# Four modulation chunks on ScalarE's queue, constants in two transfers, and matmuls in TensorE's early waits

## The reference

```python
mod = silu_c @ w_ada[l] + b_ada[l]
mod_ctx = silu_cc @ w_ada[l] + b_ada[l]
sh1, sc1, g1, sh2, sc2, g2 = jnp.split(mod[:, None, :], N_ADA, axis=-1)
...
u_ctx = _modulate(_rms_norm(ctx, norm1_g[l]), sh1c, sc1c)
hc_f, hc_b = _bidir_rglru(u_ctx @ w_in[l][:, :D_LRU], *lru_p, h_zero, h_zero)
...
u = _modulate(_rms_norm(x, norm1_g[l]), sh1, sc1)
mix, _, _ = _mixer(u, rows, h0_f, h0_b, w_in[l], ...)
x = x + g1 * mix
x = x + g2 * _swiglu(_modulate(_rms_norm(x, norm2_g[l]), sh2, sc2), w_ffn_in[l], w_ffn_out[l])
return _rms_norm(x, norm_f_g)
```

## Time and profile before

| | us |
|---|---|
| median of three runs | 2579.61 |
| the profiled execution's own time | 2582.47 |
| its span, first to last instruction | 2580.7 |
| TensorE busy in the span | 2552.7 (99%) |
| VectorE busy | 1983.7 (77%) |
| ScalarE busy | 1220.8 (47%) |

### The profile page before, as it was taken

How to read it: one execution, slowest core, us unless ns; L and a number is a source line. 1 busy time by engine, 2 the same in 40 slices (tenths; PEclk the granted TensorE clock), 3 DMA queues, 4 the chain that set the end, 5 groups by cost and what they waited for, 6 DMA issues and landing times.

```text
span 2580.7 us, 39175 instructions
## 1 busy us (share of the span) xinstructions
PE 2552.7 (99%) x14527; PEld 2197.5 (85%) x14527; DVE 1983.7 (77%) x2223; ACT 1220.8 (47%) x1422; POOL 205.5 (8%) x277
## 2 busy tenths in 40 slices
PE   7999999999999999999999999999999999999998
PEld 6888888878888888888888888888888888888887
DVE  5567998778999999877967878777877767787443
ACT  4224887355555555422444444444444445455433
POOL 0010000000001111111000000000000000011000
PEclk8999999999999999999999999999999999999999
DMA  9985444755556666999668888888888864756644
GB/s 353 355 316 187 131 132 150 270 198 159 159 162 160 166 156 149 323 334 337 176 156 203 203 199 204 202 201 200 205 202 200 207 236 148 164 125 179 218 158 153
DMA packets 540412, 524.81 MB, mean 203 GB/s; under 512 B 16472, under 2 KB 491424, under 8 KB 535584
## 3 DMA queue, kind: packets, MB, share of 16 engines
q1 hardware_dynamic: 491296, 379.17, 47.8%
q0 software_dynamic: 44176, 126.90, 21.0%
q10 hardware_dynamic: 4848, 17.47, 1.7%
HBM read 427.00 MB, written 54.53 MB: 187 GB/s over the span
## 4 chain that ended last, share of the span: by engine, by line
PE 93%; DVE 3%; DMA 2%; ACT 1%; issue 1%; ACTq 0%; SPq 0%; DVEq 0%
PE main L1758 17%; PE aux L1758 17%; PE main L1765 9%; PE aux L1765 9%; PE main L1471 7%; PE main L1472 7%; PE main L1473 7%; PE aux L1999 3%; PE aux L1998 3%; PE aux L2000 3%; DMA ada_pa<-in_w_ada 1%; PE aux L1521 1%; PE main L1999 1%; PE main L2000 1%; PE main L1998 1%; PE aux L1471 1%
## 5 line engine op out<-in xcount | busy, mean ns | idle before, releaser
L2478 DVE TENSOR_TENSOR l_S<-f_S,h_S 128x1024 fp32r<-128x1024 f32 x288 | 344.9, 1219 | 15.3 <-ACT h_S L1056 15.3
L2478 DVE TENSOR_TENSOR l_A<-f_A,h_A 128x1024 fp32r<-128x1024 f32 x216 | 263.3, 1221 | 101.8 <-ACT h_A L1056 87.8
L1056 ACT ACTIVATE h_A<-f_A 128x1024 fp32r<-128x1024 f32 x216 | 226.6, 1051 | 221.2 <-PE aux L1765 111.6
L1056 ACT ACTIVATE h_S<-f_S 128x1024 fp32r<-128x1024 f32 x288 | 288.8, 1052 | 72.6 <-DVE f_S L2466 47.3
L1471 PE MATMUL main<-u_both,w_hi 128*128 128x512 f32 (+1 forms) x528 | 207.9, 394 | 0.3 <-DVE ctx_lo L2213 0.2
L1758 PE MATMUL main<-t_both,h_S 128*128 128x512 f32 x864 | 207.9, 389 | 0.2 <-DVE u_hi_spare L2531 0.2
L1758 PE MATMUL aux<-t_both,h_S 128*128 128x512 f32 x864 | 207.8, 389 | 0.0
L1472 PE MATMUL main<-u_both,w_hi 128*128 128x512 f32 (+1 forms) x528 | 203.7, 386 | 0.0
L1473 PE MATMUL main<-u_both,w_lo 128*128 128x512 f32 (+1 forms) x528 | 203.1, 385 | 0.0
L2126 DVE TENSOR_TENSOR w_lo<-w_raw,w_hi 128x1024 fp32r<-128x1024 f32 x120 | 146.0, 1221 | 64.7 <-ACT w_hi L826 64.5
L826 ACT ACTIVATE w_hi<-w_raw 128x1024 fp32r<-128x1024 f32 x120 | 125.8, 1053 | 147.6 <-DMA w_raw<-in_w_out 60.9
(11 more groups left out here) (363 smaller groups left out, 5637.1 us busy)
## 6 DMA issues: line engine op xcount, KB each, us to landing
f_A<-in_w_ffn_in SPq DMA_DIRECT2D x120, 512.0 KB, 5.3
f_S<-in_w_ffn_in SPq DMA_DIRECT2D x80, 512.0 KB, 5.7
f_S<-f_A POOLq DMA_DIRECT2D x80, 512.0 KB, 6.4
f_A<-in_w_in SPq DMA_DIRECT2D x72, 512.0 KB, 4.9
ada_pq<-in_w_ada SPq DMA_DIRECT2D x64, 512.0 KB, 8.5
ada_pw<-in_w_ada POOLq DMA_DIRECT2D x64, 512.0 KB, 6.2
bw_f<-in_w_ffn_out SPq DMA_DIRECT2D x56, 512.0 KB, 7.1
w_raw<-in_w_in SPq DMA_DIRECT2D x48, 512.0 KB, 4.7
```

The costliest lines, as they stand in the source:

```text
L1056: act.activation(wh[v][:, :, :], wf[b][v][:, :, :], ACT.Copy).then_inc(w_hi_done, 1)
L2478: dve.tensor_tensor(wl[b][v][:, :, :], wf[b][v][:, :, :], wh[v][:, :, :].bitcast(F32), ALU.subtract).then_inc(w_lo_done, 1)
```

## The change

**Chunks.** The first four chunks no longer come through GpSimd's queue into `ada2_pa`. ScalarE issues their transfers, before `hi` of unit 8, as soon as the last piece is used, into a new tile `ada2_pl` over the second half of the ring of pieces. GpSimd issues chunks 4 to 31, the first four of them without waiting for a free slot. VectorE takes chunks 0 to 3 from `ada2_pl`; the edges of `pad` rows 4 to 7 are cleared, and those rows written, only after chunk 3 is used.

**Constants.** The identity (64 KB) is loaded first; the other 256 KB are loaded by SP just ahead of the store of x. Their readers wait for the second transfer.

**Matmuls in the waits.** `keep_warm(n)` issues n float32 matmuls of 256 columns into a free accumulator; nobody reads what they write. Nine stand among pieces 3, 4 and 5.

```diff
--- before.py
+++ after.py
@@ -59,7 +59,7 @@
 EARLY_CHUNKS = {8: 5, 9: 5, 10: 5, 11: 5, 12: 4, 13: 4, 14: 4, 15: 0}
 N_EARLY = 32
 N_MID = N_EARLY + 16
-LANDED = (20 * 16, 20 * 16, 12 * 16, 12 * 16)
+LANDED = (19 * 16, 19 * 16, 11 * 16, 11 * 16)
 
 
 NPAIR = D_FF // P
@@ -249,6 +249,7 @@
         xcv_l = sb("xcv_l", "ada", [TCAT], F32R, 3 * kb)
         dft_t = sb("dft_t", "mix", [3, T], F32, 16 * kb)
         ada2_pa = sb("ada2_pa", "yx", [4, 1024])
+        ada2_pl = sb("ada2_pl", "lru", [4, 1024], F32, 16 * kb)
         ada2_pc = sb("ada2_pc", "pf", [2, 1024])
         ada2_pw = sb("ada2_pw", "u_hi", [4, 1024], F32, 16 * kb)
         ada2_acc = sb("ada2_acc", "ada", [1024], F32, 8 * kb)
@@ -437,7 +438,7 @@
                 unit(0, 8, 0, u, in_t[:, UC * q:UC * q + UC, j * UN:j * UN + UN])
 
 
-            sp.dma_start(const[:, :], consts).then_inc(const_landed, 16)
+            sp.dma_start(const[:, 0:P], consts[:, 0:P]).then_inc(const_landed, 16)
             for i in range(4):
                 sp.dma_start(x_tok[:, i, :], x[0, P * i:P * i + P, :]).then_inc(rows_landed[i], 16)
             for i in range(2):
@@ -447,6 +448,7 @@
                 for u in EARLY_UNITS.get(n, ()):
                     xa_unit(u)
             sp.wait_ge(raw_out, 16)
+            sp.dma_start(const[:, P:], consts[:, P:]).then_inc(const_landed, 16)
             sp.dma_start(x_fm, x_raw[:, :, :]).then_inc(x_stored, 16)
             for u in range(8, 16):
                 xa_unit(u)
@@ -756,8 +758,8 @@
 
             pool.wait_ge(x_stored, 16)
             pool.wait_ge(u_aff, 2 * KT)
-            for n in range(N_EARLY):
-                if n >= 4:
+            for n in range(4, N_EARLY):
+                if n >= 8:
                     pool.wait_ge(ada2_used, n - 3)
                 chunk(n, ada2_pa[:, n % 4, :])
             for n in range(N_EARLY, N_MID):
@@ -889,6 +891,9 @@
                 act.activation(pad[:, 4 * i + 2 * j:4 * i + 2 * j + 2, PADX:PADX + T], main[:, 2 * j:2 * j + 2, :],
                                ACT.Copy).then_inc(pair_free[j], 1)
 
+            act.wait_ge(ada_used, 32)
+            for n in range(4):
+                act.dma_start(ada2_pl[:, n, :], ada_t[:, n, 2 * D:2 * D + 1024]).then_inc(ada_landed[n], 16)
             hi(0, 8, 0, 8)
             hi(0, 8, 0, 9)
             xa_out(0, 0)
@@ -896,6 +901,7 @@
             for u in range(8, 16):
                 hi(0, 8, 0, u + 2)
                 if u % 4 == 3:
+                    act.wait_ge(ada2_used, 4)
                     xa_out(1, u // 4 - 2)
             sums_evac(2, 2, sums_row)
 
@@ -1590,10 +1596,22 @@
             ins.then_inc(rstd_spread, 1)
             pe.wait_ge(cvec_ready, 1)
 
-            for n in range(4):
+            pe.wait_ge(raw_out, 24)
+
+            def keep_warm(n):
+
+                for _ in range(n):
+                    pe.matmul(main[:, 3, 0:256], ones[:, :], x_raw[:, 0, 0:256], start=True, stop=True)
+
+            for n in range(3):
                 ada_piece(n)
+            keep_warm(3)
+            ada_piece(3)
+            keep_warm(1)
             turn_row(0)
+            keep_warm(2)
             ada_piece(4)
+            keep_warm(3)
             for n in range(5, 32):
                 ada_piece(n)
                 xa_half(n - 5, n // 4 if n % 4 == 3 else None)
@@ -1664,12 +1682,14 @@
             def middle_channels():
 
                 pe.wait_ge(branch_out, 4)
+                pe.wait_ge(const_landed, 32)
                 for g in range(4):
                     ins = pe.matmul(aux[0:1, 3, g * P:g * P + P], yx[:, 12 + g, TH:TH + 1], cs128[:, 0:P], start=True, stop=True)
                 ins.then_inc(chunk_ready, 1)
 
             def channels(t):
                 pe.wait_ge(side_rows_done, 5)
+                pe.wait_ge(const_landed, 32)
                 pe.wait_ge(branch_out, 7 + t)
                 for g in range(4):
                     for odd in range(2):
@@ -1680,7 +1700,7 @@
 
             def tokens(t):
                 if t == 0:
-                    pe.wait_ge(const_landed, 64)
+                    pe.wait_ge(const_landed, 80)
                     pe.wait_ge(row_out, len(RANGES) + 2)
                 pe.wait_ge(pair_free[t], Q_FOUR // 2 + 1)
                 for g in range(4):
@@ -2136,9 +2156,12 @@
                     ins = dve.scalar_tensor_tensor(acc[:, :], src, k, acc[:, :], ALU.mult, ALU.add)
                 ins.then_inc(ada2_used, 1)
 
-            def chunk_next(n, src, acc=None):
-                dve.wait_ge(ada2_landed[n % 4], 16 * (n // 4 + 1))
-                chunk(src, n, cvec[:, n % 16, 0:1], acc)
+            def chunk_next(n, acc=None):
+                if n < 4:
+                    dve.wait_ge(ada_landed[n], 32 * 8 + 16)
+                else:
+                    dve.wait_ge(ada2_landed[n % 4], 16 * (n // 4))
+                chunk(ada2_pl[:, n, :] if n < 4 else ada2_pa[:, n % 4, :], n, cvec[:, n % 16, 0:1], acc)
 
             def mod2_out(a, b, n, bank):
 
@@ -2239,14 +2262,22 @@
 
 
             dve.wait_ge(ada_used, 32)
-            dve.memset(pad[:, :, 0:2], 0.0)
-            dve.memset(pad[:, :, 2 + TC:PADX], 0.0)
-            link(dve.memset(pad[:, :, PADX + T:PADX + T + 1], 0.0))
+            def clear_edges(rows):
+                dve.memset(pad[:, rows, 0:2], 0.0)
+                dve.memset(pad[:, rows, 2 + TC:PADX], 0.0)
+                link(dve.memset(pad[:, rows, PADX + T:PADX + T + 1], 0.0))
+
+            clear_edges(slice(0, 4))
 
             def xa_out(i, j):
                 dve.wait_ge(unit_used, 7 + j if i == 0 else 8 + 4 * j + 4)
                 dve.tensor_copy(pad[:, 4 * i + 2 * j:4 * i + 2 * j + 2, 2:2 + TC],
                                 aux[:, j, :].rearrange("p (n t) -> p n t", t=TC)).then_inc(ctx_free[j], 1)
+
+            def early_chunks(u):
+                done = sum(EARLY_CHUNKS[v] for v in range(8, u))
+                for n in range(done, done + EARLY_CHUNKS[u]):
+                    chunk_next(n, ada2_acc1 if n // 16 == 1 else ada2_acc)
 
             lo(0, 8, 0, 8)
             lo(0, 8, 0, 9)
@@ -2254,9 +2285,10 @@
             xa_out(0, 1)
             for u in range(8, 16):
                 lo(0, 8, 0, u + 2)
-                done = sum(EARLY_CHUNKS[v] for v in range(8, u))
-                for n in range(done, done + EARLY_CHUNKS[u]):
-                    chunk_next(n, ada2_pa[:, n % 4, :], ada2_acc1 if n // 16 == 1 else ada2_acc)
+                early_chunks(u)
+                if u == 8:
+                    dve.wait_ge(ada2_used, 4)
+                    clear_edges(slice(4, 8))
                 if u % 4 == 3:
                     xa_out(1, u // 4 - 2)
 
@@ -2345,7 +2377,7 @@
                     if u in (1, 2):
                         if first and u == 1:
                             dve.wait_ge(acc_used, 1)
-                        dve.wait_ge(ada2_landed[u - 1], h * 16 + (4 * N_EARLY + 16))
+                        dve.wait_ge(ada2_landed[u - 1], h * 16 + 4 * N_EARLY)
                         chunk(ada2_pc[:, u - 1, :], h * 2 + (N_EARLY + u - 1),
                               cvec[:, ds(h * 2 + (u - 1), 1), 0:1].rearrange("p o n -> p (o n)"))
                     if u == 3:
@@ -2370,6 +2402,7 @@
             def pool_group(g):
 
                 if g == 0:
+                    dve.wait_ge(const_landed, 32)
                     dve.memset(pw_b[:, :, :], 0.0)
                 dve.memset(pw_a[:, :, 0:8], 0.0)
                 dve.memset(pw_a[:, :, 72:80], 0.0)
```

## The result

Timed with the kernel before on one chip, the changed kernel takes **2592.15 us** (median of 6 runs, 2591.37 to 2593.89), the kernel before 2579.89 (6 runs, 2579.2 to 2581.19). The ratio is 1.0047, interval 1.0037 to 1.0056: slower by 12.3 us. The forecast was slower, 2586.5 us; the time lies above its range. The profiled execution took 2591.37 us, its span is 2589.6.

What follows compares the result with a forecast made beforehand. Bound by TensorE until its last piece, by the chunks at 215 us, with unit 9's landing equally tight. 8.8 + 1.8 - 2.0 - 1.7 = +6.9 on 2582.47 gives 2589.4, less 2.86 to the median: 2586.5 us; range 2575.5 to 2589.5.

Steps and rivals of the forecast that it cites:

- Which transfer is tight: Before TensorE's unit 8: unit 9's landing at 142.2 us has about 0.1 us to spare; delays move TensorE one for one.
- The signs named for a right forecast: In the profile: ScalarE waiting until about 150, TensorE idle 7 to 11 us, SP's queue at a quarter of the bytes.
- No wait is left: 2.0 + 1.7 return: Before the partition sums at 215 us: the wait for VectorE and the half clock after it vanish, -3.7 us.
- the clock: After TensorE's idle stretch before unit 8: half clock was to cost 1.8 us.
- Matmuls in the waits and constants at 0: At the start: up to 2.65 us of lead at 46 us, hidden behind unit 9's transfer, costed at 0.
- 8.8 us of delay: At unit 9's landing: both sets of four chunks pass nearly wholly first, moving it from 142.2 to 151.0 us.
- the equal turns: In the transfer engines: queues alternate single packets, so the weights' queue with 1 KB rows gets a quarter of the bytes.
- The bound below: At unit 9: its last packets go before any chunk packet, and it lands at 142.2 us as now.
- Rival (b): At unit 9: only ScalarE's set interferes, delay 5.6, +3.7 us, 2583.3; chance 0.27 with (c) and delays between.
- Rival (a): Chunks wait until the weights are through: -3.7 to -2.2 us; chance 0.15, plus 0.08 with the early lead added.
- Rival (c): Unit 9 in time, unit 10 up to 5.6 us late; wait at 215 us grows 2.4: 2582.0; 0.27 with (b).
- my estimate by it: At unit 9: four bursts of weights meet four and about two of chunks, delay near 7.5 us, sum 1.3 us smaller.

Runs made afterwards that it cites:

- experiment 1: The kernel before, unedited, in a second profiled execution: 2581.13 us, span 2579.4.
- experiment 2: The kernel before with the constants in two transfers and the nine added matmuls, without the chunks: 2580.75 us, ratio 1.0003.
- experiment 4: The changed kernel with ScalarE's four chunk issues moved behind its conversions of units 8 and 9: 2581.65 us, ratio 1.0005.
- experiment 12: The changed kernel with units 8 and 9 ahead of the store, constants' second part behind unit 11, ScalarE's issues behind its two conversions: 2580.02 us, ratio 1.0.
- experiment 3: The kernel before with only the four chunks on ScalarE's queue: median 2581.06 us, 10 runs from 2580.02 to 2590.19, ratio 1.0013.
- experiment 5: The changed kernel with the constants in one transfer again: 2588.62 us, ratio 1.0034.
- experiment 6: The changed kernel without the added matmuls: 2591.83 us, ratio 1.0046.
- experiment 9: The changed kernel with ScalarE's four issues held behind one added copy: 2582.94 us, ratio 1.0011.
- experiment 7: The changed kernel with GpSimd's chunks 4 to 7 held until unit 9 has landed: 2588.38 us, ratio 1.0032.
- experiment 10: The changed kernel with ScalarE's four issues held behind three added copies: 2583.87 us, ratio 1.0013.
- experiment 8: The changed kernel with units 8 and 9 ahead of the store of x and the constants' second part behind unit 11: 2581.87 us, ratio 1.0008.

## Why the prediction was wrong

**Which transfer is tight: right.** Unit 9 was named as the transfer with about 0.1 us to spare, and a delay was to move TensorE one for one. Its landing was forecast for 151.0 and came at 151.5; unit 8 for 154.2, and it started at 154.54; chunk 0 for 156.4, and it ran at 156.87. The signs named for a right forecast are there, all but one: ScalarE's wait, the standstill of 7 to 11 us, half clock behind it, none at 44 us, no wait before the sums. The exception: SyncE's queue was to have a quarter of the bytes, and had 0.09 of 1.22 MB, 7%, from 141 to 144 us and 0.19 of 1.20 MB, 16%, from 145 to 148.

**The step that failed: "No wait is left: 2.0 + 1.7 return".** No wait is left, as forecast, but the term was mis-sized: 3.7 us in the sum, 0.5 measured. The stall of 2.01 us and its half clock were real in the one trace at hand, but the execution of experiment 1 had 0.5 and none. Nor has the typical execution 3.7 us to give: experiments 2, 4 and 12 have no wait before the sums, and their medians are 0.7, 1.6 and 0.1 us above those of before. The hint stood in the prediction itself: that execution was 2.86 us above the median of its runs. I moved the sum to the median by subtracting this whole excess, and credited the 3.7 us as well. As far as the excess was the stall, the same microseconds were counted twice; that all of it was is not shown, since the execution of experiment 1, almost without the stall, is only 1.34 us shorter. With 0.5 for the term the forecast is 2586.5 + 3.7 - 0.5 = 2589.7, and 0.9 more for the clock (2.7 instead of 1.8) gives 2590.6, against 2592.15 measured. The traces do not account for the remaining 1.5 us: the two profiled executions differ by 10.24 us and the medians by 12.3.

**Matmuls in the waits and constants at 0: right alone, wrong together with the chunks.** Alone they change nothing clear of the noise (experiment 2), for the reason given. But the prediction wrote the lead into ScalarE's issues ("now about 1 us sooner") and did not ask what that would decide. It did: the chunks alone, at 138.2, mostly win the race, and at 137.0 to 137.6 they lose it in all runs (experiment 3 against 5, 6 and the kernel after). That 8.8 us of delay were forecast and 8.3 came is therefore in part luck. The forecast put the issues at 138.5, and they came at 137.03; issues at 138.18 cost experiment 3 nothing in most runs, and at 139.71 they cost experiment 9 only 2.6 us of unit 9's landing. And the equal turns from which the 8.8 was worked out are not what the rows show.

**The bounds and rivals.** The bound below, unit 9 not delayed at all, was not idle: it is what experiment 3 shows in most of its runs. Rival (b), ScalarE's set alone, was not what happened, but what experiment 7 made happen, at 5.3 to 6.5 us where it had 5.6. Rival (a) gave -3.7 to -2.2 us for a won race. Experiments 3 (in most runs), 4 and 12 won it and gained nothing that can be measured: the wait that they were to remove was 0.5 in experiment 1. Rival (c), unit 9 in time and unit 10 late, came in the trace of experiment 3, where unit 10 landed at 154.3 instead of 150.7; its price did not come, for the wait before the sums was 0.4 us there.

**Turns of the queues.** From 141 to 144 us 93 weight packets passed beside 307 chunk packets, not one for one. Two readings fit. By row, a chunk packet takes 0.938 x 48 / 307 = 147 ns of an engine and a weight packet 0.088 x 48 / 93 = 45 ns. An engine that alternates would do 15.6 of each in 3 us: six engines in turns and ten with chunks alone give 94 and 298. Or all engines take three chunk packets to one of the weights. From 145 to 148 us SyncE's and GpSimd's queues stand at 182 to 184, which the first reading explains without more. The rows do not part them. Nor do equal counts, as in the earlier trace rows, show that turns are of single packets: turns of equally many packets at a time give the same. The Trainium skill (DMA: Bandwidth & Descriptors, Queues, rings and completion order) has an engine change queues only after a packet of about 9 to 17 descriptors; my estimate by it was a delay near 7.5 us, the measured one is 8.3 (experiment 2 to the kernel after). That is nearer to the forecast's 8.8, but no run here was made to decide it.

**Still open**: why experiment 3 loses in some runs (no trace caught a lost one), and which packets meet on the slowest engine. The race itself is shown by issue times and landings, not by packets: the first chunk packets pass at 139.2 to 139.5 us in the kernel after and in experiment 3 alike, 2.2 us behind the issue in the one and 1.0 in the other (experiment 10's expectation has 1.5 to 2 in every trace), and from 139 to 141 us there are 81 of them in the one and 59 in the other.

## What to carry to other kernels

A wait that one trace shows is worth what it is in the typical execution: where the profiled one lies above the median, ask first whether the stall is that excess, and never credit the stall and subtract the excess both. Before moving transfers to a free queue, look at which small-packet transfer is still under way in the engines when they arrive; large rows from a second queue can hold its last packets back for as long as the whole new set takes, so issue them behind the landing that TensorE waits for. An edit that is worth nothing alone still moves issue times: price it again for every race that it shifts.

## What the runs showed of the hardware

- Two outcomes of one program: the chunks alone gave 2580.0 to 2581.2 us in six runs and 2584.1 to 2590.2 in four, while the kernel before stayed within 2579.1 to 2582.2 in the 27 runs beside them.
- How far the chunks' first issue lies ahead of the landing of the store of x goes with what they cost: 1.6 us ahead, unit 9 landed 3.2 us behind the store; 1.9 ahead, 4.2; 2.5 ahead, 8.3; 3.1 ahead, 11.4; without chunks 2.7.
- Three issues of ScalarE took 1.42 us in the kernel after and 4.55 us in experiment 8, and its conversions stood behind them. An issue can hold its engine.
- After the standstill of 9.4 us in the kernel after, the granted clock was 0.50, TensorE's 1.2 GHz level, for 5.5 us of work, and TensorE's shift grew by 2.7 us. It grew by 2.8 after 6.6 us in experiment 7, by 1.5 after 5.7 us in experiment 5 and by 1.7 after 2.5 us in experiment 10. The 2.7 us of experiment 9, the 1.4 of experiment 8 and the 0.9 of experiments 2 and 4 were followed by no half clock: the length of a wait alone does not tell.
